# Mixture of experts: the experts' rows are summed into the tokens by matrix products on chip, in plain fp32, in place of a scatter to HBM and a read back

## The reference

```python
x = x + token_mixer(rmsnorm(x, norm_mix_g), ...)
h = rmsnorm(x, norm_ffn_g)
# 4 groups of 8 experts; each token takes its best group and 2 experts in it, with weights w_tok (T, 2)
for each expert e, for the rows of h that chose e:          # 32 experts, 1024 (token, expert) pairs in all
    y = (silu(rows @ w_e_gate[e]) * (rows @ w_e_up[e])) @ w_e_down[e]   # 1024 -> 512 -> 1024
x = x + sum over a token's two experts of weight * y
x = rmsnorm(x, norm_final_g)
```

## Time and profile before

| | |
|---|---|
| median of 3 runs | 1799.57 us (1795.98 to 1802.8) |
| the profiled execution's own time | 1800.18 us |
| its span in the trace | 1798.3 us |
| instructions | 21260 |
| PE busy | 1661.2 us (92%) |
| DVE, ACT, POOL busy | 747.4, 615.1, 133.9 us |
| HBM read, written | 317.97 MB, 14.69 MB |

### The profile page before, as it was taken

One profiled execution on the slowest core, in us unless ns is written; L12 is line 12 of the kernel. 1 busy time (PEld: TensorE's weight loads), 2 busy tenths in 40 slices (PEclk: granted clock), 3 DMA queues, 4 the chain that ended last, 5 costly groups with the idle time before them and its releaser, 6 DMA issues.

```text
span 1798.3 us, 21260 instructions
## 1 busy us (share of the span) xinstructions
PE 1661.2 (92%) x8323; PEld 1215.3 (68%) x8323; DVE 747.4 (42%) x1398; ACT 615.1 (34%) x1073; POOL 133.9 (7%) x199
## 2 busy tenths in 40 slices
PE   6999999999999798898778877899999999999899
PEld 5888888888888643333323333688788888988677
DVE  3544345544564521010101012772646643446782
ACT  4122225444441411111111112655353232457760
POOL 0000001001000001111111110010011000000320
PEclk9999999999999899999999998999999999999999
DMA  7665364653226779999999998233123342322102
GB/s 151 88 102 95 105 94 71 67 65 61 68 106 241 276 300 426 427 426 427 427 427 426 428 425 309 103 98 102 35 70 94 94 142 87 98 70 92 54 2 70
DMA packets 115123, 325.91 MB, mean 181 GB/s; under 512 B 8213, under 2 KB 81685, under 8 KB 102224
## 3 DMA queue, kind: packets, MB, share of 16 engines
q1 hardware_dynamic: 109232, 313.76, 52.3%
q0 software_dynamic: 4784, 8.13, 1.2%
q10 hardware_dynamic: 1008, 2.65, 0.4%
HBM read 317.97 MB, written 14.69 MB: 185 GB/s over the span
## 4 chain that ended last, share of the span: by engine, by line
PE 37%; DMA 14%; ACT 2%; DVE 2%; issue 1%; SPq 0%; ACTq 0%; DVEq 0%; POOL 0%; POOLq 0%
DMA up<-in_w_e_up 13%; PE bank L1424 7%; PE bank L1426 7%; PE bank L1425 7%; PE bank L1732 3%; PE turned L1424 2%; PE turned L1425 2%; PE turned L1426 2%; PE bank L1505 1%; PE bank L1758 1%; PE bank L1870 1%; PE bank L1964 1%; PE bank L1539 1%; PE turned L1505 1%; DMA y_tok<-y_dram 0%
## 5 line engine op out<-in xcount | busy, mean ns | idle before, releaser
L2004 DVE TENSOR_TENSOR w_lo<-w_raw,w_hi 128x2048 fp32r<-128x2048 f32 (+1 forms) x72 | 156.8, 2179 | 288.5 <-ACT w_hi L912 279.1
L912 ACT ACTIVATE w_hi<-w_raw 128x512 fp32r<-128x512 f32 (+3 forms) x138 | 169.6, 1252 | 291.6 <-DMA w_raw<-in_w_in 103.6
L1732 PE MATMUL bank<-gate,xt 128*64 128x512 f32 x512 | 225.4, 593 | 25.0 <-DMA up<-in_w_e_up 25.0
L1733 PE MATMUL bank<-up,xt 128*64 128x512 f32 x512 | 225.9, 594 | 0.0
L2326 DVE TENSOR_TENSOR gated_h<-gu_silu,bank 64x512 f32<-64x512 f32 x32 | 22.1, 690 | 391.3 <-ACT gu_silu L1126 391.3
L1732 PEld LDWEIGHTS bank<-gate,xt 128*64 128x64 f32 x512 | 68.6, 137 | 165.1 <-issue 165.1
L1424 PE MATMUL bank<-h1T_hi,w_hi 128*128 128x512 f32 x376 | 151.0, 402 | 0.0
L1758 PE MATMUL bank<-down,hT 128*64 128x512 f32 x256 | 129.8, 655 | 22.2 <-DVE hT L2333 22.2
L1426 PE MATMUL bank<-h1T_hi,w_lo 128*128 128x512 f32 x376 | 146.9, 391 | 0.0
L1425 PE MATMUL bank<-h1T_lo,w_hi 128*128 128x512 f32 x376 | 146.6, 390 | 0.0
L1759 PE MATMUL bank<-down,hT 128*64 128x512 f32 x256 | 129.8, 655 | 0.0
(11 more groups left out here) (691 smaller groups left out, 3659.2 us busy)
## 6 DMA issues: line engine op xcount, KB each, us to landing
down<-in_w_e_down SPq DMA_DIRECT2D x32, 2048.0 KB, 35.6
up<-in_w_e_up SPq DMA_DIRECT2D x30, 2048.0 KB, 38.0
gate<-in_w_e_gate SPq DMA_DIRECT2D x30, 2048.0 KB, 33.3
w_raw<-in_w_in SPq DMA_DIRECT2D x24, 1024.0 KB, 10.0
w_raw<-in_a_w_in SPq DMA_DIRECT2D x20, 1024.0 KB, 5.4
w_raw<-in_w_in SPq DMA_DIRECT2D x16, 512.0 KB, 10.5
w_raw<-in_a_w_out SPq DMA_DIRECT2D x8, 1024.0 KB, 5.1
w_raw<-in_w_conv_out SPq DMA_DIRECT2D x4, 1024.0 KB, 5.1
```

The source lines that it names most:

```text
L912: return nc.scalar.activation(out, in_, ACT.Copy, scale=scale)
L1732: g_ins = pe.matmul(out[0:CAP, :], x, ring_gate[p][:, c, :], start=c == 0, stop=c == KC - 1)
L1733: u_ins = pe.matmul(out[CAP:, :], x, ring_up[p][:, c, :], start=c == 0, stop=c == KC - 1)
L2004: V.tensor_tensor(ring_view(w_lo, n), ring_view(raw, n), ring_view(w_hi, n).bitcast(F32), ALU.subtract)\
```

## The change

The result rows no longer go to HBM. ACT writes them, already multiplied by their weight (`slot_w`, a column for each expert), into `y_s`: 128 slots of a pair by 1024 columns. For each pair, DVE makes `hot_tok`, a table of ones of 128 slots by 512 tokens. PE multiplies it with `y_s` in 8 products (`sums`: four tiles of 128 tokens by two halves of 512 columns, each of 128 slots), plain fp32. DVE adds each result, from PSUM, to `x1_tok` (`adds`).

The sums of pair q stand in expert 2q+2: three among its last three gate/up chunks, three behind them, two between `h_turn` and `down`. The last pair's stand behind the loop. They rotate through five banks (4, 5, 7, 0, 3), so gate/up has bank 2 alone and down bank 6. The slots' weights are made once, in expert 0, by 24 small products (`slot_weights`); SP waits for them before the load of `gfin`, and so before the loads of expert 3. Scatters, `y_dram`, the read back and the diagonal tables are gone. The last low part `w_lo` of the first weight slice behind the loop goes from DVE to POOL.

```diff
-        gu_bank = lambda e: bank[(2, 4)[e % 2]]
-        y_number = lambda e: (6, 7)[e % 2]
-        y_bank = lambda e: bank[y_number(e)]
+        gu_bank = lambda e: bank[2]
+        y_bank = lambda e: bank[6]
+        tile_half = lambda k: (k // 2, slice(512 * (k % 2), 512 * (k % 2) + 512))
+        def sum_bank(q, k):
+            return bank[LAST_BANKS[k] if q == NE // 2 - 1 else SUM_BANKS[(SUMS * q + k) % len(SUM_BANKS)]]
...
             sp.wait_ge(sem("over_made"), 1)
+            sp.wait_ge(sem("slot_w_summed"), 1)
             sp.dma_start(gfin[:, :], t["norm_final_g"].unsqueeze(0).to_broadcast([P, D])).then_inc(gfin_loaded, 16)
...
-            sp.wait_ge(moe_done, 1)
-            y_v = y_dram[0:TOPK * SEQ, :].rearrange("(k t p) d -> k p t d", k=TOPK, p=P)
-            for tt in TILES2:
-                sp.dma_start(y1_tok[:, tt, :], y_v[0, :, tt, :]).then_inc(sem(f"y1_loaded{tt}"), 16)
-                sp.dma_start(y2_tok[:, tt, :], y_v[1, :, tt, :]).then_inc(sem(f"y2_loaded{tt}"), 16)
...
-                put(2 * q - 2)
-                put(2 * q - 1)
-            put(NE - 2)
...
+            pool.wait_ge(w_hi_made, splits_before(slices1) + 1)
+            nc.gpsimd.tensor_tensor(ring_view(w_lo, slices1), ring_view(raw, slices1), ring_view(w_hi, slices1).bitcast(F32), ALU.subtract)\
+                .then_inc(w_lo_made, 1)
...
-                copy(ys[e % 2][:, 0:512], y_bank(e)[0:CAP, :])
-                copy(ys[e % 2][:, 512:1024], y_bank(e)[CAP:, :]).then_inc(y_made, 1)
+                copy(y_s[rows, 0:512], y_bank(e)[0:CAP, :], slot_w[0:CAP, e:e + 1]).then_inc(sem("last_left_made") if e == NE - 1 else y_made, 1)
+                if e < NE - 1:
+                    copy(y_s[rows, 512:1024], y_bank(e)[CAP:, :], slot_w[CAP:, e:e + 1]).then_inc(y_made, 1)
...
+            def sums(q, ks):
+                for k in ks:
+                    tt, cols_ = tile_half(k)
...
+                    if q < NE // 2 - 1 and SUMS * q + k >= len(SUM_BANKS):
+                        pe.wait_ge(sem("added"), SUMS * q + k - len(SUM_BANKS) + 1)
+                    who = hot_tok[:, tt * P:(tt + 1) * P]
+                    pe.matmul(sum_bank(q, k)[:, :], who, y_s[:, cols_], start=True, stop=True).then_inc(sem("summed"), 1)
+
             for e in range(NE):
-                gate_up(e, range(KC))
-                if e % 2 == 1 and e + 1 < NE:
-                    x_turn(e // 2 + 1)
-                h_turn(e)
+                if e % 2 == 0 and e >= 2:
+                    q = e // 2 - 1
+                    gate_up(e, range(5))
+                    for c in range(5, KC):
+                        sums(q, [c - 5])
+                        gate_up(e, [c])
+                    sums(q, (3, 4, 5))
+                    h_turn(e)
+                    sums(q, (6, 7))
+                else:
+                    gate_up(e, range(KC))
+                    if e == 0:
+                        slot_weights()
+                    elif e + 1 < NE:
+                        x_turn(e // 2 + 1)
+                    h_turn(e)
                 down(e)
...
-            idle_turns(bank[6], 22)
...
-            pe.wait_ge(sem("x2_made"), 2 * TT - 2)
-            idle_turns(bank[6], 24)
+            idle_turns(bank[1], 4)
+            sums(NE // 2 - 1, range(SUMS))
+            pe.wait_ge(sem("x2_gained"), TT - 1)
+            idle_turns(bank[4], 24)
...
+            def adds(q, ks):
+                for k in ks:
+                    tt, cols_ = tile_half(k)
+                    dve.wait_ge(sem("summed"), SUMS * q + k + 1)
+                    V.tensor_tensor(x1_tok[:, tt, cols_], x1_tok[:, tt, cols_], sum_bank(q, k)[:, :], ALU.add).then_inc(sem("added"), 1)
+
             for e in range(NE):
-                gated(e)
-                if e % 2 == 1 and e + 1 < NE:
-                    x_copy(e // 2 + 1)
-                h_copy(e)
+                q = e // 2
+                if e % 2 == 0 and e >= 2:
+                    adds(q - 1, range(3))
+                    gated(e)
+                    adds(q - 1, (3,))
+                    h_copy(e)
+                    adds(q - 1, range(4, SUMS))
...
+            for tt in range(TT):
+                adds(NE // 2 - 1, (2 * tt, 2 * tt + 1))
+                dve.wait_ge(sem("added"), SUMS * (NE // 2 - 1) + 2 * tt + 2)
+                V.tensor_tensor(x2g_tok[:, tt, :], x1_tok[:, tt, :], gfin[:, :], ALU.mult).then_inc(sem("x2_gained"), 1)
```

More of the change, by code:

```diff
@@ L351, in build_kernel @@
         xg = at("xg", [2 * CAP, D], F32, BASE + 2 * BIG)
[L352 removed]
+        y_s = at("y_s", [P, D], F32, BASE + 2 * BIG + 8192)
+        hot_tok = temp("hot_tok", 8)
+        all_tok = temp("all_tok", 7)
+        hot_w = temp("hot_w", 4, (P, TOPK * TT, NBLK))
+        over_y = big("over_y", 2, shape=(CAP, D))
+        over_hot = temp("over_hot", 0, (CAP, SEQ))
         gu_silu = at("gu_silu", [P, FE], F32, BASE + 2 * BIG + 4096)
@@ L832, in _ @@
             get_pair(1)
[L833 to L836, removed]
-                put(2 * q - 2)
-                put(2 * q - 1)
-            put(NE - 2)
-            put_rows_of(NE - 1)
+            for q in range(1, NE // 2 - 1):
+                pool.wait_ge(x_turned, q + 1)
+                get_pair(q + 1)
             count, _ = over_values(pool)
-            pool.wait_ge(y_made, NE)
-            scatter(1)
             pool.wait_ge(gathered, 16 * (NE // 2 - 1))
-            pool.wait_ge(scattered, 16 * (NE + 2))
+            pool.wait_ge(sem("last_left_made"), 1)
+            pool.wait_ge(sem("last_right_made"), 1)
             nc.gpsimd.memset(pool_mark[:, 0:1], 0).then_inc(sem("ovf_free"), 1)
@@ L1768, in _, with slot_weights @@
             ins.then_inc(results, 1)
-            for e in range(NE):
-                gate_up(e, range(KC))
-                if e % 2 == 1 and e + 1 < NE:
-                    x_turn(e // 2 + 1)
-                h_turn(e)
+            def slot_weights():
+                pe.wait_ge(sem("hot_w_made"), 1)
+                for b, slots in enumerate((hot_slot, hot_back)):
+                    for q in range(TOPK * TT):
+                        pe.matmul(turns_of(bank[5][0:CAP, 0:NE], b), slots[:, q, :], turns_of(hot_w[:, q, 0:NE], b),
+                                  start=q == 0, stop=q == TOPK * TT - 1)
+                for q in range(TOPK * TT):
+                    ins = pe.matmul(bank[5][0:CAP, NE:NBLK], hot_slot[:, q, :], hot_w[:, q, NE:], start=q == 0, stop=q == TOPK * TT - 1)
+                ins.then_inc(sem("slot_w_summed"), 1)
@@ new lines, in _ @@
+                        dve.wait_ge(sem("ovf_rows"), i * 3 + 3)
+                        V.tensor_scalar(over_hot[:, :], all_tok[0:CAP, :], over_col[:, 0:1], None, ALU.is_equal).then_inc(sem("ovf_hot"), 1)
+                        for a in range(2):
+                            dve.wait_ge(sem("ovf_summed"), i * 2 + a + 1)
+                            for tt in range(TT):
+                                part = x1_tok[:, tt, 512 * a:512 * a + 512]
+                                ins = V.tensor_tensor(part, part, bank[SUM_BANKS[tt]][:, :], ALU.add)
+                            ins.then_inc(sem("ovf_added"), 1)
```

169 lines of the change are left out of this document (83 added, 86 removed).

## The result

The changed kernel takes 1853.4 us (median of 4 runs, 1850.42 to 1855.73), the kernel before 1799.51 us beside it (4 runs). The ratio is 1.029, with a 95% interval from 1.028 to 1.031: slower, by 54 us. The forecast was slower by 33 us, 1833, with 1848 as the upper end of its range. The sign and the main mechanism hold; the time lies above the range. The trace is of an execution of 1855.73 us, the slowest of the four.

A forecast was written before the change was run, and what follows sets the result against it. PE, limiting only the loop's first part before, was to limit all of it: sums and switches +84.6, expert 0 +1.4, vanished waits -41.5, behind the loop -11.1, together +33.4 us, giving 1833, range 1815 to 1848.

The forecast's parts named there:

- The sign: Whole kernel: the change makes it slower, with a chance of 0.88.
- the main mechanism: Experts' loop: PE sets its whole pace, at 31.3 to 33 us a pair; chance 0.80.
- What bounds the kernel: Experts' loop before: PE up to expert 13, weights' transfer from 14; afterwards PE throughout, waits for weights vanishing, -41.5 us.
- The rival in which the transfer still sets the loop: Experts' loop: sums fill PE's spare 4.2 us a pair, if adding less than 3.6; 1779 us, faster; chance 0.07.
- The sums' cost: PE, even experts: eight fp32 products, 6.88 us a pair, 2.24 covered by gaps, so 4.64 more.
- The switches: PE, half-width to full-width products and back: 0.10 us each, ten a pair, 1.0 us, bounds 0 and 1.6.
- The clock: PE in the loop: low clock at downs after gaps, none forecast since sums fill even experts' gaps; all back, +12 us.
- a rival at 0.08: A new wait or the clock: late gated_h, or a full drain (+9) with slow stretches (+12); past 1848 us; chance 0.08.
- What hides beside it: Loop: DVE's adds (5.5 us a pair), single banks for gate/up and down, SP's wait (some 3 us) delay nothing.
- POOL's low part: Behind the loop: takes 5.2 us on POOL, ready near 9, wanted after 25, so hidden.
- Behind the loop: From last down to last gain: 14.0 us in place of 25.1, so -11.1, between -9 and -12.
- The sum: Whole kernel: +44.5 for the loop and -11.1 behind it, +33.4 us, giving 1833.

The follow-up runs named there:

- no_sums: Changed kernel without the sums and adds of the first 15 pairs, whose rows are missing from the result: 1788.6 us, ratio 0.993.
- two_parts_block: Changed kernel with each sum as two fp32r products in place of one fp32, and all gate/up chunks ahead of the sums: 1790.6 us, ratio 0.995.
- one_block: Changed kernel with all gate/up chunks first, then the sums; four passages a pair in place of ten: 1832.4 us, ratio 1.018.
- three_together: Changed kernel with three sums together between chunks 6 and 7, so six passages a pair in place of ten: 1845.3 us, ratio 1.025.
- fill_gaps: Changed kernel with idle turns in the gaps of expert 0 and the odd experts: 1846.8 us, ratio 1.026.
- late_low: Changed kernel with POOL's subtraction for w_lo started only after DVE's four gains: 1855.4 us, ratio 1.030.
- more_turns: Changed kernel with 36 idle turns in place of 24 ahead of the next layer's turns: 1851.8 us, ratio 1.029.
- fill_down: Changed kernel with 7 idle turns ahead of down in odd experts 1 to 29 only: 1849.0 us, ratio 1.027.
- all_together: two_parts_block with SP's wait and gfin's load moved behind expert 28, fill_gaps' turns, w_hi and w_lo made in expert 30, 36 idle turns: 1789.0 us, ratio 0.993.

## Why the prediction was right and wrong

**What bounds the kernel.** Right. Experts 0 to 13 never waited for a weight, and the sums made PE the limit of the whole loop; no wait for weights is left. The rival in which the transfer still sets the loop needed less than 3.6 us of sums a pair. It is what no_sums shows from expert 16 on; two_parts_block, at half the price a product, waits for weights once, at expert 30. The forecast named both the point and the condition.

**The sums' cost.** Right in its main term: 8 products, 6.88 us a pair, 2.24 of them in covered gaps. 14.28 forecast from the expert's start to down, with 1.0 for passages 15.3; measured 15.9 (669.86 to 685.76), the difference being the passages.

**The switches: this step failed in size.** "I take 0.10 each way" counted the first late start of a passage alone. The start after it is late as well, by 0.10 into a full-width product and 0.05 out of one. one_block and three_together give 0.17 a passage around the chunks, and the ten of a pair cost 1.6 us (32.88 - 26.63 - 4.64): the upper bound that the prediction named. +9.2 us. The bound had come from the 0.16 by which a record outlasts the next start; that the two sizes agree is shown, that the one causes the other isn't.

**The clock: this step failed.** "The gaps of even experts are filled with sums, so I forecast none." The odd experts and expert 0 kept theirs, and six downs ran slowly, +10.2 us in the profiled execution. With the gaps filled (fill_gaps) none is slow, and the loop is 10.2 shorter. But they aren't sufficient: one_block has the same gaps and not one slow down, and late_low and more_turns, with the changed kernel's own loop, have four. No filled gap was followed by a slow down, in fill_gaps, fill_down and all_together alike, which speaks for the gaps as the condition; which unfilled gap tips the clock, and why as many as six did here, stays open. The prediction had the price (12 for all of it) and put it into a rival at 0.08. The error was to let the filling of half the gaps stand for all of them.

**What hides beside it.** Right for the adds, the banks and SP's wait: no sum, no `gated_h` of an even expert and no load came late. **Wrong for POOL's low part**, "hidden". Nothing waits for it, but DVE loses 2.7 us beside it, and 3.1 if it is moved (3.26 against 0.17). Being off the path by its result, it was on it by what it did to its neighbour. The Trainium skill's SBUF — State Buffer, section "Who interferes with whom", has this: a DVE instruction with two inputs from SBUF, or one in a two-port mode, shuts out or is shut out by a POOL instruction that reads SBUF, whichever comes second, and for its whole length. The rows of the changed kernel agree: the gain has both inputs in SBUF and ends 1.1 us behind POOL, and the adds, with one input from PSUM, ran beside POOL in 1.45 for two. Whether late_low's operation of four columns, which has one input, was in a two-port mode no row shows. The forecast had not weighed it.

**Behind the loop.** -11.1 forecast, -9.3 measured: the 2.7 of this stall, less 0.9 by which the rest was better. The turns after it took 2.8 longer, at a clock of 0.50 and then 0.76; the forecast had left the clock there as before.

**The sum.** In the span, 1853.6 measured and 1831.7 forecast: 21.9 missing. Passages 9.2, clock in the loop 10.2, POOL's stall 2.7 less 0.9, turns 2.8; less 1.0 for the start and 1.0 for the rest: 22.0. The range was too narrow because it joined the full price of the passages only with half of the slow stretches, and had no term for the turns. In the medians 20.4 are missing (1853.4 against 1833).

## What to carry to other kernels

Where a stage seems to be set by a transfer, see in its first half whether the other engine ever waited for it. Deep buffers hide an engine that is the limit, and work put on it then counts in full. Small products that use the array in another shape belong in one block: a change of shape cost up to 0.17 us here, so ten in a pair were 1.6 us and four 0.6 (31.84 - 26.63 - 4.64). Before a product is called cheap, count its records: one fp32 product with a table of ones cost 0.86 us, two fp32r ones 0.46, and this turned +3% into +0.6%, with the sums in one block into -0.5%. Work that is moved into a loop because an engine is idle there may have to wait for a transfer, and then holds up what stands behind it.

## What the runs showed of the hardware

- Late starts after a change of shape come in twos (0.10 and 0.10 us into the full-width product, 0.10 and 0.05 out of it). On a change of tiling mode, the Trainium skill's TensorEngine Tiling (Array Packing), section "Key Properties", says that it drains TensorE. The trace agrees in sign, with 0.17 us a passage; that this is the time of a drain no row shows.
- POOL's fp32 subtraction of 128 × 2048 (4.5 us) held one DVE instruction until about its end, one of 1024 columns (3.90 against 1.23) as well as one of four (3.26 against 0.17).
- Gaps of 0.3 and 0.9 us in dense work are followed in some experts by some 3 us at the lower clock, in the changed kernel at every eighth expert from 3 to 27, and in others not; kernels with the same loop have six, four and four such downs. With idle turns in the gaps there was none, and the turns cost nothing (loop 521.0 us, which is 531.2 less 10.2).
- With 0.4 to 2.0 us of idle time ahead of them the next layer's turns ran at the full clock in six kernels, with 2.3 to 7.8 us more slowly in eight.
